# Two token halves in the first job of a mixer, attention and feed-forward kernel on one core

## What is computed

```python
def rmsnorm(x, g):
    xf = x.astype(jnp.float32)
    y = xf * lax.rsqrt(jnp.mean(xf * xf, axis=-1, keepdims=True) + EPS)
    return (y * g.astype(jnp.float32)).astype(x.dtype)
...
    h = h + hybrid_mixer(rmsnorm(h, mix_norm[l]), w_in[l], conv_w[l], ...)
...
    proj = u @ w_in
    z, xbc, dt_raw, v = jnp.split(proj, [...], axis=-1)
    xbc = jax.nn.silu(causal_depthwise_conv(xbc, conv_w, conv_b)).astype(jnp.float32)
```

## Time and profile before

| | us |
|---|---|
| time, median of 3 runs | 1694.58 |
| its lowest and highest run | 1693.11 to 1694.98 |
| the profiled execution: time | 1694.56 |
| the profiled execution: span of the trace | 1692.8 |
| PE busy in the span | 1663.4 (98%) |
| DVE, ACT, POOL busy | 916.9 (54%), 572.4 (34%), 1053.0 (62%) |
| granted TensorE clock, mean | 0.998 of full speed |

### The profile page before, as it was taken

How to read it: one execution, slowest core, us unless ns; L and a number is a source line. 1 busy time by engine, 2 the same in 40 slices (tenths; PEclk the granted TensorE clock), 3 DMA queues, 4 the chain that set the end, 5 groups by cost and what they waited for, 6 DMA issues and landing times.

```text
span 1692.8 us, 22289 instructions
## 1 busy us (share of the span) xinstructions
PE 1663.4 (98%) x8073; PEld 1364.6 (81%) x8073; DVE 916.9 (54%) x1411; ACT 572.4 (34%) x990; POOL 1053.0 (62%) x779
## 2 busy tenths in 40 slices
PE   7999999999999999999999999999999999999997
PEld 5897997888878888888888888887878777777785
DVE  5323948782445222221247997998475784443416
ACT  5331248330422100100144445756131345553203
POOL 7676754476647766766774889782577544333563
PEclk9999999999999999999999999999999999999999
DMA  6333333223343323333233332221423321121221
GB/s 207 125 102 121 104 100 125 96 79 100 100 149 94 92 93 95 99 100 100 81 117 101 99 100 90 77 83 54 162 72 106 95 75 51 51 74 51 75 87 50
DMA packets 191274, 162.10 MB, mean 96 GB/s; under 512 B 9684, under 2 KB 187472, under 8 KB 190672
## 3 DMA queue, kind: packets, MB, share of 16 engines
q1 hardware_dynamic: 190984, 160.84, 30.5%
q10 hardware_dynamic: 200, 0.06, 0.0%
HBM read 155.60 MB, written 4.23 MB: 94 GB/s over the span
## 4 chain that ended last, share of the span: by engine, by line
PE 92%; DVE 4%; ACT 2%; POOL 1%; issue 1%; DMA 0%; DVEq 0%; SPq 0%; ACTq 0%
PE g_bank L888 65%; PE g_bank L905 7%; PE g_bank L915 6%; PE t_bank L1465 2%; PE t_bank L1475 2%; PE g_bank L1369 1%; PE t_bank L1205 1%; PE t_bank L1237 1%; PE t_bank L1287 1%; PE t_bank L1308 1%; PE g_bank L1351 1%; PE t_bank L1454 1%; PE t_bank L949 1%; PE t_bank L1445 1%; DVE t_bank L2647 0%
## 5 line engine op out<-in xcount | busy, mean ns | idle before, releaser
L751 POOL TENSOR_TENSOR w_lo<-w_raw,w_hi 128x512 fp32r<-128x512 f32 x392 | 541.1, 1411 | 8.2
L738 POOL TENSOR_SCALAR w_hi<-w_raw 128x2048 fp32r<-128x2048 f32 x98 | 192.6, 1965 | 497.4 <-issue 214.0
L888 PE MATMUL g_bank<-x_hi,w_hi 128*128 128x512 f32 x1248 | 494.8, 396 | 0.2 <-DVEq L2222 0.2
L888 PE MATMUL g_bank<-x_hi,w_lo 128*128 128x512 f32 x1248 | 486.0, 389 | 0.0
L888 PE MATMUL g_bank<-x_lo,w_hi 128*128 128x512 f32 x1248 | 486.0, 389 | 0.0
L888 PEld LDWEIGHTS g_bank<-x_hi,w_hi 128*128 128x128 f32 x1248 | 234.4, 188 | 52.1 <-issue 4.4
L888 PEld LDWEIGHTS g_bank<-x_hi,w_lo 128*128 128x128 f32 x1248 | 234.3, 188 | 49.2
L888 PEld LDWEIGHTS g_bank<-x_lo,w_hi 128*128 128x128 f32 x1248 | 234.5, 188 | 48.5 <-issue 1.7
L2647 DVE SCALAR_TENSOR_TENSOR t_bank<-hc,cols,t_bank 128x512 f32<-128x512 f32 x280 | 187.0, 749 | 4.7 <-DVE hc L2631 2.8
L799 POOL TENSOR_TENSOR w_lo<-w_raw,w_hi 128x512 fp32r<-128x512 f32 x104 | 134.3, 1324 | 68.1 <-ACT w_hi L1868 68.1
L888 PE MATMUL g_bank<-y_hi,w_hi 128*128 128x512 f32 x332 | 130.9, 394 | 0.0
(11 more groups left out here) (458 smaller groups left out, 2907.3 us busy)
## 6 DMA issues: line engine op xcount, KB each, us to landing
w_raw<-w_gate_up SPq DMA_DIRECT2D x44, 512.0 KB, 5.0
w_raw<-a_w_in SPq DMA_DIRECT2D x44, 512.0 KB, 4.5
w_raw<-b_w_in SPq DMA_DIRECT2D x38, 512.0 KB, 4.3
w_raw<-w_in SPq DMA_DIRECT2D x28, 512.0 KB, 4.8
w_raw<-w_kv SPq DMA_DIRECT2D x16, 512.0 KB, 4.4
w_raw<-w_out_mix SPq DMA_DIRECT2D x16, 512.0 KB, 6.3
w_raw<-w_down SPq DMA_DIRECT2D x16, 512.0 KB, 3.9
w_raw<-a_w_out SPq DMA_DIRECT2D x16, 512.0 KB, 4.0
```

Source lines behind the costliest of these rows:

```text
L738: nc.gpsimd.tensor_scalar(w_hi[:, par], w_raw[:, par], 1.0, 0.0, ALU.mult, ALU.add).then_inc(pool_chain, 1)
L751: last = nc.gpsimd.tensor_tensor(w_lo[:, par, s], w_raw[:, par, s], w_hi[:, par, s].bitcast(F32), ALU.subtract)
L888: last = nc.tensor.matmul(g_bank[:, 2 * pair + f, 0:n], ww[:, k0 + k, ws], xk, start=(k == 0 and q == 0), stop=(k == kt - 1 and q == 2))
```

## The change

Job 0 is multiplied for tokens 0 to 255, and then for tokens 256 to 511. SP starts the loads as x 0, x 1, weights of job 0, x 2, x 3, weights of job 1. The transposes `xn_T(i)` take two columns k of two token tiles: i of 0 to 3 are the first half, i of 4 to 7 the second, so each still fills a bank. ACT's and DVE's `hi_of_x(i)` and `lo_of_x(i)` are two instructions of 128x256 each, instead of one of 128x512. DVE scales tiles 1, 2 and 3, ACT only tile 0. In the table of tasks three transposes now stand ahead of `params0`.

```diff
-    [("params0", 1), ("xn", DT), ("params1", 2), ...
+    [("xn_a", 3), ("params0", 1), ("xn_b", 5), ("params1", 2), ...
...
-            for kind, i in FRONT[:2]:
-                front_load(kind, i)
+            for n in range(2):
+                load_x(2 * n)
+                load_x(2 * n + 1)
+                front_load(*FRONT[n])
...
+            def xn_T(i):
+
+                h, k0 = i // 4, 2 * (i % 4)
+                if i % 4 == 0:
+                    pe.wait_ge(xn_ready, 2 * h + 2)
+                b = bank(xn_task(i))
+                for kk in range(2):
+                    for m in range(2):
+                        last = nc.tensor.transpose(b[:, (2 * kk + m) * P:(2 * kk + m + 1) * P],
+                                                   xn_nat[:, 2 * h + m, (k0 + kk) * P:(k0 + kk + 1) * P], ident[:])
+                last.then_inc(t_ready, 1)
+
+            for i in range(3):
+                xn_T(i)
             pe.wait_ge(in_small[0], 16 * len(PARAM_SETS[0]))
             n = SET_ROWS[0]
             nc.tensor.transpose(bank(TASKS["params0"])[:, 0:n], p_rows[0:n, 0, :], ident[0:n, 0:n]).then_inc(t_ready, 1)
-            pe.wait_ge(xn_ready, TT)
...
-            for k in range(4):
-                xn_T(k)
+            xn_T(3)
...
-                    for k in range(KT):
...
+                    for h in range(2):
+                        t = slice(2 * P * h, 2 * P * (h + 1))
+                        for k in range(KT):
+                            if h == 0 and k in (0, 2, 4):
+                                pe.wait_ge(w0_part, k // 2 + 1)
+                            elif h == 0 and k == 6:
+                                slot(j, j % 2, None)
+                            pe.wait_ge(nlo_ready, 4 * h + k // 2 + 1)
+                            for f in range(2):
+                                ws = slice(f * P, (f + 1) * P)
+                                for q, (ww, xx) in enumerate(((wts[0], x_hi), (wts[0], x_lo), (wts[1], x_hi))):
+                                    last = nc.tensor.matmul(g_bank[:, 2 * (j % 2) + f, t], ww[:, k, ws], xx[:, k, t],
+                                                            start=(k == 0 and q == 0), stop=(k == KT - 1 and q == 2))
+                            if h == 0 and k >= 5:
+                                for i in ((4, 5), (6,), (7,))[k - 5]:
+                                    xn_T(i)
...
             x_deviation(0)
             x_deviation(1)
             x_scaled(0)
-            x_deviation(2)
-            x_scaled(1)
-            x_deviation(3)
-            x_scaled(2)
             i = TASKS["params0"]
             link(copy(cols[:, 0:SET_ROWS[0]], ready(i)[:, 0:SET_ROWS[0]]))
...
+            hi_of_x(0)
+            x_deviation(2)
+            hi_of_x(1)
+            hi_of_x(2)
+            x_deviation(3)
+            for i in range(3, 8):
+                hi_of_x(i)
...
+            x_squares(0)
+            x_squares(1)
+            x_root(0)
+            x_normal(1)
             link(v.memset(raw[:, :, 0:PAD], 0.0))
+            x_squares(2)
             dve.wait_ge(cols_ready, 1)
...
+            lo_of_x(0)
+            x_squares(3)
+            lo_of_x(1)
+            x_normal(2)
+            lo_of_x(2)
+            x_normal(3)
+            for i in range(3, 8):
+                lo_of_x(i)
```

More of the change, by code:

```diff
@@ L120, in units_of, with xn_task @@
     return [u for u, s in enumerate(SLOT_OF) if s == n]
+def xn_task(i):
+    return TASKS["xn_a"] + i if i < 3 else TASKS["xn_b"] + i - 3
 def logit_banks(u):
@@ L552, in stream, with load_x @@
                     one(base + i, (base + i) % 2, i * step)
-            for m in range(TT):
+            def load_x(m):
                 sp.dma_start(x_nat[:, m, :], A["x"][0][m * P:(m + 1) * P, :]).then_inc(in_x[m], 16)
@@ L766, in _ @@
                 if j == KV_AT[0]:
-                    pool.wait_ge(t_ready, TASKS["xn"] + DT)
+                    pool.wait_ge(t_ready, xn_task(DT - 1) + 1)
                 if j in KV_BY_ACT:
@@ L1565, in x_scaled, with hi_of_x @@
                 copy(xn_nat[:, m, :], x_nat[:, m, :], mstat[:, 16 + m:17 + m]).then_inc(xn_ready, 1)
+            def hi_of_x(i):
+                h, b = i // 4, ready(xn_task(i))
+                for kk in range(2):
+                    k = 2 * (i % 4) + kk
+                    ins = copy(x_hi[:, k, 2 * P * h:2 * P * (h + 1)], b[:, 2 * P * kk:2 * P * (kk + 1)], col["mix_norm"](k))
+                ins.then_inc(nhi_ready, 1)
             x_deviation(0)
@@ L1577, in _ @@
             act.nop().then_inc(cols_ready, 1)
-            for k in range(DT):
-                b = ready(TASKS["xn"] + k)
-                copy(x_hi[:, k, :], b, col["mix_norm"](k)).then_inc(nhi_ready, 1)
+            hi_of_x(0)
[5 more added lines that the diff above has]
+                hi_of_x(i)
             act.wait_ge(in_mem1, 16)
@@ L2262, in x_root, with x_squares @@
                 done(v.reciprocal(mstat[:, 16 + m:17 + m], mstat[:, 12 + m:13 + m]), x_rstd)
-            for m in range(TT):
+            def x_squares(m):
                 dve.wait_ge(in_x[m], 16)
@@ L2267, in _, with x_normal, lo_of_x @@
                                             mstat[:, 8 + m:9 + m]), x_squared)
-                if m:
-                    x_root(m - 1)
-            x_root(TT - 1)
-            v.tensor_scalar(xn_nat[:, 3, :], x_nat[:, 3, :], mstat[:, 19:20], None, ALU.mult).then_inc(xn_ready, 1)
+            def x_normal(m):
+                x_root(m)
+                v.tensor_scalar(xn_nat[:, m, :], x_nat[:, m, :], mstat[:, 16 + m:17 + m], None, ALU.mult).then_inc(xn_ready, 1)
+            def lo_of_x(i):
+                r, h = xn_task(i), i // 4
+                b = ready(r)
+                dve.wait_ge(nhi_ready, i + 1)
+                for kk in range(2):
+                    k, t = 2 * (i % 4) + kk, slice(2 * P * h, 2 * P * (h + 1))
+                    ins = v.scalar_tensor_tensor(x_lo[:, k, t], b[:, 2 * P * kk:2 * P * (kk + 1)], col["mix_norm"](k),
+                                                 x_hi[:, k, t].bitcast(F32), ALU.mult, ALU.subtract)
+                done(ins, nlo_ready, t_free[BANK[r]])
+            x_squares(0)
+            x_squares(1)
+            x_root(0)
+            x_normal(1)
             link(v.memset(raw[:, :, 0:PAD], 0.0))
+            x_squares(2)
             dve.wait_ge(cols_ready, 1)
-            for k in range(DT):
-                r = TASKS["xn"] + k
-                b = ready(r)
-                dve.wait_ge(nhi_ready, k + 1)
-                done(v.scalar_tensor_tensor(x_lo[:, k, :], b, col["mix_norm"](k), x_hi[:, k, :].bitcast(F32), ALU.mult, ALU.subtract),
-                     nlo_ready, t_free[BANK[r]])
+            lo_of_x(0)
[6 more added lines that the diff above has]
+                lo_of_x(i)
             dve.wait_ge(mem1_sq, 1)
```

7 lines of the change are left out of this document (1 added, 6 removed).

## The result

The changed kernel takes **1696.74 us** (median of 20 runs, 1696.09 to 1698.19) where the kernel before, in 20 runs beside it, takes 1694.79 (1693.11 to 1695.14). The ratio is 1.0014, 95% interval 1.0007 to 1.002: 1.95 us slower, less than the 0.2% that the prediction called no change. The forecast was 1696.6. The profiled execution has a span of 1694.8, which is 2.0 more than before.

A forecast was written before the change was run, and what follows sets the result against it. PE was taken as the bound, so job 1's start counts: DVE's row with three 0.5 us port waits moves it from 29.18 to 31.2. Thus 1694.58 + 2.0 = 1696.6 us, with an 8-in-10 range of 1693.8 to 1699.4.

The forecast's parts named there:

- Arrivals: Loads at the front: job 0's weights complete near 9.3, third x at 10.8, fourth at 12.3; POOL starts 3.0 us earlier.
- The start: Ahead of job 0: PE turns x at 8.7, DVE's first pair starts at 13.1, job 0 near 15.1 against 15.72.
- x 0 and x 1 come as before: First loads: the first two tiles of x arrive unchanged, with ACT's scaling of tile 0 ending at 8.64.
- DVE's row: DVE's pairs, squares, roots and scalings from 13.1, with three port waits of 0.5, run to 22.0, when the second half turns.
- Half an instruction: Wait of each of three DVE instructions for a POOL instruction in progress at the shared port: 0.5 us each.
- the third rival: Whole waits at the port, above all tile 3's scaling meeting the 1.91 us rounding: +5.0, 1699.6; chance 0.12.
- PE behind it: Job 0's second half: turned from 22.0, its 48 products at 0.12 take 5.76 and end at 31.2, 2.0 us later.
- The price of the halves: Splitting job 0's matmuls costs 0.36 us: 96 products at 0.12 for 48 at 0.2325.
- So the 0.4 us wait remains: Behind job 0: the memory's chain is 1.9 later and PE 2.0, so PE still waits 0.4 us for DVE's scaling.
- Everything after moves along: Rest of the kernel behind job 0: all of it shifts by the same delay as the front, 2.0 us.
- PE as the bound: DVE keeps up at the front, so PE sets job 1's start at 29.2: -0.3, 1694.3; chance 0.20.
- The clock: PE's bursts leave it at the lower clock, second-half products at 0.215: 4.6 more, +6.6, 1701.2; chance 0.06.

The follow-up runs named there:

- e5: Changed kernel with POOL rounding job 1's weights in four instructions of 128x512 instead of one of 128x2048; 1696.24 us, ratio 1.0013.
- e6: Kernel before with only job 0's products made in two halves of tokens, nothing else moved; 1694.93 us, ratio 1.0006.
- e3: Changed kernel with the parameter table turned ahead of x, ACT scaling tiles 2 and 3, and `hi_of_x(1)` ahead of `x_deviation(2)`; 1693.85 us, ratio 0.9998.
- e1: Changed kernel with the transpose of the parameter table ahead of the first three transposes of x; 1695.82 us, ratio 1.0012.
- e4: Changed kernel with the loads in the old order, all four tiles of x before the weights; 1696.61 us, ratio 1.0012.
- e9: Kernel before with useless identity transposes on PE, 22 ahead of the parameter table and 18 behind it; 1694.1 us, ratio 0.9998.
- e7: Kernel before with five useless products on PE ahead of job 0; 1695.03 us, ratio 1.0006.
- e12: Changed kernel with 24 chained empty instructions in DVE's program, at its fourth step of the convolution; 1695.55 us, ratio 1.0007.
- e11: Changed kernel with useless identity transposes on PE, 22 ahead of x's first turns and 20 behind the parameter table; 1695.02 us, ratio 1.0003.
- e2: Changed kernel with tiles 2 and 3 scaled by ACT instead of DVE, the roots staying on DVE; 1696.11 us, ratio 1.0009.

## Why the prediction was right

The number was right to 0.14 us, with a chance of 0.78 on no measurable change and a delay as the likeliest case. Step by step:

- **Arrivals**: right. POOL at 9.23 (9.3 forecast), the third x at 10.53 (10.8).
- **The start**: 0.4 late. PE turned at 9.15 (8.7), since ACT's scaling ended later ("x 0 and x 1 come as before" was wrong by 0.37 for x 1), so `lo` 0 was at 13.54 (13.1) and the first product at 15.03 (15.1).
- **DVE's row**: right in what it rests on, and as a sum by some luck. The pairs cost 1.11 to 1.15 for 1.26, so the walk without waits is 6.8 (13.54 to 21.83 less 1.5) for 7.4. The waits were to be 0.5 each, 1.5 together. They were 0, 0 and 1.5. "Half an instruction" was an average over phases, and this kernel has one phase; that both come to 1.5 is luck, as is that the late start (0.4) and the cheaper pairs (0.6) nearly cancel. Two of the three instructions took their lone durations, which for all three was a sign of being wrong. The scaling of tile 3 met the long rounding, the event of the third rival, but alone. e5 shows the mechanism and its price.
- **PE behind it**: right. The second half's turns at 21.96 (22.0), job 1 at 31.02 (31.2). The 1.84 is the forecast's term of 2.0. The Trainium skill's 0.109 for a product ("TensorE: Matmul & The Clock Gate", section "Wait — 56ns, not 53.3ns?") would have made the second half 5.2; the trace has 5.83 for 48, 0.12 each, and the measurement decides.
- **The price of the halves**: 0.58 in e6 for the 0.36 worked out. The 0.12 was right. The 0.2325 for a product of 512 columns holds up to 25.3; the last sixteen stand 0.227 apart (25.32 to 28.95), so that the steady rows cost 0.42 more. The slow start, 0.15, the term left out.
- **"So the 0.4 us wait remains"**: wrong. It vanished: DVE began the two scalings of `mem` 1.7 later than before, but they took 3.19 together, where the earlier trace rows gives 4.0. "Everything after moves along" was wrong as well. Some 1.1 of the 1.84 was gone by 327, in three waits that PE had before, and 1.2 came back at 352 by the instruction pause. Two unforeseen terms of opposite sign cancel, so that 2.0 at the front and 2.0 at the end agree partly by luck: with DVE's program 24 instructions longer the same change is worth +0.9 (1695.55) and not +2.0.
- **The rivals.** PE as the bound did not come about; e3 shows it, once DVE's scalings are gone. The clock was half right. It fell after PE's pause of 2.6 us and rose in the middle of the first half, as the granted clock in windows of the changed kernel shows (window, length, busy time and instructions of PE, PEld, DVE, ACT, POOL, then the clock, DMA share, GB/s):

```profile
14.00:15.00 1.00, 0.38 (x3) 0.38 (x4) 0.72 (x3) 1.00 (x3) 0.92 (x3) 1.00 1.03 403
15.00:16.00 1.00, 1.00 (x8) 1.00 (x7) 0.93 (x2) 0.03 (x1) 1.00 (x1) 0.63 1.02 410
16.00:18.00 2.00, 2.00 (x12) 2.00 (x11) 1.46 (x4) 1.02 (x3) 1.92 (x3) 0.50 0.46 131
18.00:19.00 1.00, 1.00 (x7) 1.00 (x7) 1.00 (x3) 0.00 (x0) 1.00 (x1) 0.67 0.43 30
19.00:20.00 1.00, 1.00 (x11) 1.00 (x10) 0.61 (x3) 0.00 (x0) 1.00 (x2) 1.00 0.30 87
```

It was 0.5 (1.2 GHz) from 16 to 18, with products 0.21 apart, and 1.00 (2.4 GHz) behind 19. PE still had to wait 0.88 for DVE behind the first half, so this cost nothing, and by 25.4 the clock was up, as the forecast had it. In e1, e3, e4 and e5 the products stand 0.21 apart too, while their rows of the clock say 1.00: the distance from start to start is the surer sign.

**What stays open.** Why e9's 1.4 in the trace is 0.5 in the medians was not followed, nor why e5's gain is not in its median. The stretch from the last turns to the end of the span varies by itself (10.9 in e7, 11.1 before and after, 12.1 in e12), so that one profiled execution places a version no better than to about 1 us.

None of the versions beats the kernel before. e3 and e9 (both 0.9998) have the lowest ratios; the intervals of e6, e7, e11 and e12 take in 1 as well, and that of e2 ends at it.

## What to carry to other kernels

Starting the bounding engine sooner bought nothing here, because the engine that feeds it became the bound, with scalings and a sum of squares between the pieces that it delivers: walk the feeding engine's row, link by link, and mark each instruction with SBUF operands that now runs beside a busy GpSimd. Price such a meeting as nothing or the whole of the other's instruction, and look for the one long instruction in reach; cutting that one (e5) took 1.3 us off the start of job 1, though the median didn't show it. Under some 0.1% of a long program don't read a median as the worth of an edit until marks along the trace have shown where it arises: a few instructions more or less in an engine's program can move a pause of that engine to a place where it costs, and a few empty instructions tell (e12).

## What was not expected of the hardware

- A sum of squares (two operands, both the same SBUF tensor) waits for POOL as well: 1.23 alone, 1.75 to 2.35 beside it.
- After PE's pause of 2.6 us four turns ran at the upper level (0.41 from 14.62), and the products right behind them at the lower one, until 18.7. In e4, e5 and e12, whose PE did the same work and paused as long (2.56 and 2.57), the four turns took 0.76, the lower level; what makes the difference is not shown. In e2, with a second pause in that stretch, they ran there until 21.9.
- A pause of 0.3 to 0.4 us in DVE's instruction stream, tied to its place in the program, cost 1.2 us of the whole at one place and at most 0.4 one instruction on.
